# A hybrid encoder step on one core: second norm inside the output product, u tiles turned beside the queries, first norm between weight splits, bias line stored from ScalarE, four row buffers

## What is computed

```python
xn = rmsnorm(x, norm1_g)
z = xn @ w_in + b_in                      # split: attention q,k,v | mLSTM q,k,v | gates
x = x + merge(attention, mlstm, gates)    # two branch products, sigmoid gates, then @ w_out
xn = rmsnorm(x, norm2_g)
q = (xn @ peer_wq).reshape(n, 8, 2, 64)   # 8 heads, two sub keys each
s = einsum('nhpd,hpkd->nhpk', q, sub_keys)
fv, eidx = top_k of the 16 x 16 sums of the two top-16 lists    # 16 experts per head
h = gelu(u[eidx] . xn)                    # 16384 experts, u and v are 16384 x 1024
x = x + sum(softmax(fv) * h * v[eidx])
y = rmsnorm(x, final_g)
```

## Time and profile before

| | us |
|---|---|
| median of three runs | 1967.35 (1964.7 to 1967.36) |
| the profiled execution, its own time | 1964.37 |
| its span in the profile | 1962.5 |
| TensorE busy / VectorE / ScalarE / GpSimd | 1886.2 / 1371.4 / 873.8 / 848.8 |
| mean granted clock of TensorE | 0.987 |

### The profile page before, as it was taken

The page is one execution under the profiler, slowest core; times in us unless marked ns, Lnnn a source line. Parts: engine busy times, 40 slices in busy tenths (PEclk is TensorE's granted clock), DMA queues, the critical chain, the costliest instruction groups (busy, mean ns, idle before and its releaser), DMA issues. The chain is left out here.

```text
span 1962.5 us, 32250 instructions
## 1 busy us (share of the span) xinstructions
PE 1886.2 (96%) x11529; PEld 1799.0 (92%) x11529; DVE 1371.4 (70%) x2645; ACT 873.8 (45%) x1839; POOL 848.8 (43%) x670
## 2 busy tenths in 40 slices
PE   7999999998989999999999899999999999999998
PEld 6988878888979998999999899999999999999997
DVE  3126746667541898899999777775677787777775
ACT  4021122234131437688888778773333333333333
POOL 4425323331114359688888776651122222222210
PEclk9999999999989999999999999999999999999999
DMA  7632189987711445999999999999799999999982
GB/s 175 115 95 80 53 213 285 266 262 256 177 54 23 139 148 174 283 287 283 289 294 272 281 309 311 328 307 314 264 334 341 348 331 346 351 327 348 350 299 92
DMA packets 325954, 481.08 MB, mean 245 GB/s; under 512 B 37628, under 2 KB 250108, under 8 KB 322468
## 3 DMA queue, kind: packets, MB, share of 16 engines
q1 hardware_dynamic: 287724, 341.63, 56.9%
q0 software_dynamic: 36864, 134.23, 21.3%
q10 hardware_dynamic: 1208, 3.16, 0.4%
HBM read 393.81 MB, written 83.97 MB: 243 GB/s over the span
## 5 line engine op out<-in xcount | busy, mean ns | idle before, releaser
L1493 PE MATMUL ps<-x_high,split_high 128*128 128x416 f32 x1024 | 371.6, 363 | 20.6 <-DVE split_low L1480 17.9
L1493 PE MATMUL ps<-x_high,split_low 128*128 128x416 f32 x1024 | 362.9, 354 | 0.0
L1493 PE MATMUL ps<-x_low,split_high 128*128 128x416 f32 x1024 | 360.9, 352 | 0.0
L2140 PE MATMUL ps<-hid_high,split_high 128*128 128x416 f32 x1024 | 358.9, 350 | 1.5 <-PEq L1707 1.5
L2140 PE MATMUL ps<-hid_low,split_high 128*128 128x416 f32 x1024 | 358.8, 350 | 0.0
L2140 PE MATMUL ps<-hid_high,split_low 128*128 128x416 f32 x1024 | 358.7, 350 | 0.0
L1362 POOL DMA_INDIRECT gathered_rows<-in_peer_v_dram,gathered_index x128 | 134.3, 1049 | 419.6 <-DVE gathered_acc L1399 342.7
L2083 ACT CAST split_high<-area 128x1024 fp32r<-128x1024 f32 x127 | 133.3, 1049 | 383.5 <-PE ps L2140 382.7
L1684 POOL TENSOR_SCALAR area<-iota_row,chosen 128x128 f32<-128x128 f32 x240 | 287.9, 1206 | 2.1
L2111 DVE TENSOR_TENSOR split_low<-area,split_high 128x1024 fp32r<-128x1024 f32 x127 | 155.6, 1225 | 136.1 <-ACT split_high L2083 136.1
L1493 PEld LDWEIGHTS ps<-x_high,split_high 128*128 128x128 f32 x1024 | 194.0, 189 | 28.7 <-DVE split_low L1480 21.9
(11 more groups left out here) (293 smaller groups left out, 3782.4 us busy)
## 6 DMA issues: line engine op xcount, KB each, us to landing
area<-in_peer_v_dram SPq DMA_DIRECT2D x128, 512.0 KB, 5.5
u_nat<-in_peer_u_dram SPq DMA_DIRECT2D x392, 128.0 KB, 5.8
routing<-dense SPq DMA_DIRECT2D x26, 1024.0 KB, 7.2
area<-hidden SPq DMA_DIRECT2D x128, 208.0 KB, 7.1
hidden<-gelu_out SPq DMA_DIRECT2D x124, 208.0 KB, 5.1
w_raw<-in_w_in_dram SPq DMA_DIRECT2D x44, 512.0 KB, 6.1
mv_nat<-in_peer_u_dram SPq DMA_DIRECT2D x120, 128.0 KB, 3.6
u_nat<-turned_u SPq DMA_DIRECT2D x30, 512.0 KB, 3.7
```

Source lines behind the costliest of these rows:

```text
L1493: ins = self.nc.tensor.matmul(self.k.ps[:, b, 0:N], w[:, b, kk, :], x[:, kk, 0:N], start=(kk == 0 and p == 0), stop=(kk == KD - 1 and p == 2))
L2140: ins = nc.tensor.matmul(ps[:, kk, 0:N], v[:, b, kk * P:(kk + 1) * P], h[:, b, :], start=(n == 0 and p == 0), stop=(n == P - 1 and p == 2))
```

## The change

The order of `units` in the input product becomes: three tiles of x, the first product of mq, the other two tiles of x, three more products, then cache and bias line. ScalarE makes one tile's statistics after the other. The norm's weights are loaded as full rows, and the norm multiplies by them, so that turned halves need one copy and one subtraction each. Some constants are issued from ScalarE, and so are the eight stores of the bias line. In `merge` the units of the output product are ordered so that frame tiles become complete one after the other; VectorE normalises each, TensorE turns it two units later, ScalarE and VectorE split it, the splits of the first query weights stand between, and two query products are made at the block's end. In `queries` VectorE makes the low parts of the query weights, and eight more tiles of u (30 to 37) are loaded, turned and stored there. The routing matrices of ScalarE are made in place, without the tile `apart`. `RING` is 4 and `AHEAD` 38. Query weights and the split x lie at fixed places in memory.

```diff
-AHEAD = 30
+BESIDE_ATTENTION = 30
+AHEAD = BESIDE_ATTENTION + 8
...
-RING = 3
+RING = 4
...
-LOADS = QUARTERS + 2
+LOADS = 3
...
+QUERY_UNITS = [(0, 0), (1, 0), (0, 1), (1, 1)] + [(m, h) for m in range(2, PH) for h in range(2)]
+QUERIES_AHEAD = 2
...
+def query_weights_high(nc, k, pool, m):
+
+    if m % 4 == 0:
+        pool.wait_ge(k.wq_loaded[m // 4], 16 * QUARTERS)
+    if m >= 2:
+        pool.wait_ge(k.q_done, 1 + max(i for i, (b, _) in enumerate(QUERY_UNITS) if b == m - 2))
+    nc.gpsimd.tensor_copy(k.wq_high[:, m % 2], query_weights(k, m)).then_inc(k.wq_high_done, 1)
+
+
+def query_weights_low(nc, k, dve, m):
+
+    dve.wait_ge(k.wq_high_done, m + 1)
+    nc.vector.tensor_tensor(k.wq_low[:, m % 2], query_weights(k, m), k.wq_high[:, m % 2], ALU.subtract).then_inc(k.wq_low_done, 1)
...
+    def load(self, sp, n):
+
+        after(sp, self.k.u_turned, n - 1)
+        load_quarters(sp, self.nat[:, n % 2, :], self.peer_u, n, self.k.tile_loaded[3 + n % 2])
...
+    def turn(self, dve, n):
+        dve.wait_ge(self.k.tile_loaded[3 + n % 2], 16 + 16 * QUARTERS * (n // 2 + 1))
+        after(dve, self.k.u_stored[n % 2], 32 * (n // 2))
+        for i in range(2):
+            kk = slice(i * KD // 2, (i + 1) * KD // 2)
+            ins = self.nc.vector.transpose(self.turned[n % 2][i].bitcast(U32).rearrange("p (b g i) -> p g b i", b=KD // 2, i=BLK),
+                                           self.nat[:, n % 2, :].bitcast(U32).rearrange("p (g b j) -> p g b j", g=P // BLK, j=BLK)[:, :, kk, :])
+        ins.then_inc(self.k.u_turned, 1)
...
-    units = [("xn", (t, g), "vec") for t in range(NT) for g in range(2)]
-    units += [("cache", s, "act") for s in range(4)]
-    units += [("line", i, "act") for i in range(2)]
+    rest_of_x = [("xn", (t, g), "vec") for t in range(3, NT) for g in range(2)]
+    cache_and_line = [("cache", s, "act") for s in range(4)] + [("line", i, "act") for i in range(2)]
...
+        if c == 0:
+            units += new[0:1] + rest_of_x + [new[2], new[1], new[3]] + cache_and_line + new[4:]
...
+    STATISTICS_BEFORE = {("xn", (0, 0)): [0, 1, 2], ("mq", (0, 0, 0)): [3, 4]}
...
+            load_x(0)
+            sp.dma_start(g1_row, norm1_g[0].partition_broadcast(P)).then_inc(g1_loaded, 16)
+            load_x(1)
+            load_x(2)
+            load_tile(0)
+            load_x(3)
+            load_x(4)
+            load_tile(1)
+            sp.dma_start(kc_nat, cache_att_k[0, 0].rearrange("(s p) h d -> p s (h d)", p=P)).then_inc(cache_loaded, 16)
+            sp.dma_start(table[:, 0, :], att_rel_bias[0, 1:P + 1, :]).then_inc(tab_loaded, 16)
+            sp.dma_start(table[:, 1, :], att_rel_bias[0, P + 1:2 * P + 1, :]).then_inc(tab_loaded, 16)
...
-                if 5 <= i < 5 + PIECES:
-                    sp.wait_ge(line_done, 1)
-                    rows = slice((i - 5) * P // PIECES, (i - 4) * P // PIECES)
-                    sp.dma_start(k.line_dram[:, rows], bcast(line, 1, P // PIECES)).then_inc(line_stored, 16)
...
+            def statistics(t):
+                r = ROWS[t]
+                act.wait_ge(x_loaded[t], 16)
+                nc.scalar.activation(xn[0:r, t, :], x[0:r, t, :], ACT.Square, accum_out=k.ss[0:r, t:t + 1]).then_inc(k.squared, 1)
+                act.wait_ge(k.averaged, t + 1)
+                nc.scalar.activation(k.ss[0:r, t:t + 1], k.rstd[0:r, t:t + 1], ACT.Sqrt).then_inc(k.rooted, 1)
...
+                    act.dma_start(wg_raw[:, :, :], w_in[0, :, GATES:GA].rearrange("(k p) n -> p k n", p=P)).then_inc(wg_loaded, 16)
+                    act.wait_ge(tab_loaded, 48)
...
+                    nc.scalar.copy(xnT_high[:, 4 * g:4 * g + 4, t * P:t * P + r], turned_bank(u, r)).then_inc(high_out, 1)
+                if kind == "mk" and arg[1:] >= (1, 0):
+                    i = 2 * arg[1] + arg[2] - 2
+                    act.wait_ge(line_done, 1)
+                    act.dma_start(k.line_dram[:, i * P // PIECES:(i + 1) * P // PIECES], bcast(line, 1, P // PIECES)).then_inc(line_stored, 16)
+                if kind == "mv" and arg[1:] in ((0, 0), (0, 1)):
+                    i = 6 + arg[2]
+                    act.dma_start(k.line_dram[:, i * P // PIECES:(i + 1) * P // PIECES], bcast(line, 1, P // PIECES)).then_inc(line_stored, 16)
...
+                nc.vector.scalar_tensor_tensor(out=xn[0:r, t, :], in0=x[0:r, t, :], scalar=k.rstd[0:r, t:t + 1],
+                                               in1=g1_row[0:r, :], op0=ALU.mult, op1=ALU.mult).then_inc(normed, 1)
...
+    UNITS = [(i, t) for i in range(2) for t in range(NT)] + [(2, 0), (2, 1), (3, 0), (3, 1)] + [(i, t) for t in range(2, NT) for i in (2, 3)]
+    OUTS = len(UNITS)
+    ends = [UNITS.index((3, t)) for t in range(NT)]
...
+                elif c == CHUNKS - 1:
+                    pool.wait_ge(summed, 2 * KD)
+                    for m in range(2):
+                        query_weights_high(nc, k, pool, m)
+                    pool.wait_ge(out_done, NT * (c - 1 - CHUNKS // 2))
...
+            def turn(t):
+                r = ROWS[t]
+                pe.wait_ge(x_normed, t + 1)
+                for g in range(2):
+                    b = (2 * t + g) % 4
+                    after(pe, k.x_low_done, 2 * t + g - 3)
+                    for i in range(4):
+                        kk = 4 * g + i
+                        ins = nc.tensor.transpose(ps[:, b, i * P:i * P + r], xn[0:r, t, kk * P:(kk + 1) * P], ident[0:r, 0:r])
+                    ins.then_inc(k.frames_turned, 1)
+
...
+                if u - 2 in ends[0:4]:
+                    turn(ends.index(u - 2))
+            pe.wait_ge(k.x_low_done, 6)
+            for i in range(QUERIES_AHEAD):
+                pe.wait_ge(out_added, OUTS - 3 + i)
+                query(nc, k, pe, i)
+                if i == 0:
+                    turn(NT - 1)
...
+                if t >= 1:
+                    r = ROWS[t - 1]
+                    for g in range(2):
+                        act.wait_ge(k.frames_turned, 2 * (t - 1) + g + 1)
+                        nc.scalar.copy(k.x_high[:, 4 * g:4 * g + 4, (t - 1) * P:(t - 1) * P + r], turned_bank(t - 1, g)).then_inc(x_high_done, 1)
...
+                for a in range(QUARTERS):
+                    cols = slice(a * D // QUARTERS, (a + 1) * D // QUARTERS)
+                    ins = nc.vector.scalar_tensor_tensor(out=xn[0:r, t, :].rearrange("r (b a j) -> r a b j", b=KD, a=QUARTERS)[:, a],
+                                                         in0=x[0:r, t, cols].rearrange("r (b j) -> r b j", b=KD), scalar=k.rstd[0:r, t:t + 1],
+                                                         in1=g2_row[0:r, cols].rearrange("r (b j) -> r b j", b=KD), op0=ALU.mult, op1=ALU.mult)
+                ins.then_inc(x_normed, 1)
...
+                if u in (NT + 2, NT + 3):
+                    query_weights_low(nc, k, dve, u - NT - 2)
+                if u in ends:
+                    norm(ends.index(u))
+                if u == ends[2]:
+                    x_low(0)
+                if u > ends[2] and u % 2 == 0:
+                    x_low(1 + (u - ends[2]) // 2)
...
-                nc.gpsimd.tensor_tensor(w_low[:, m % 2], raw, w_high[:, m % 2], ALU.subtract
-                                        ).then_inc(w_low_done, 1)
+            for m in range(2, PH):
+                query_weights_high(nc, k, pool, m)
...
+            for n in range(BESIDE_ATTENTION, AHEAD):
+                ahead.store(sp, n)
+                if n + 2 < AHEAD:
+                    ahead.load(sp, n + 2)
...
+            later = list(range(BESIDE_ATTENTION, AHEAD))
+            for m in range(4, PH):
+                for n in later[2 * (m - 4):2 * (m - 3)]:
+                    ahead.turn(dve, n)
+                query_weights_low(nc, k, dve, m)
...
-                    after(act, second_ready, b - 1)
-                    if b - 2 in plan.on_scalar:
-                        act.wait_ge(scalar_first_ready, sum(i <= b - 2 for i in plan.on_scalar))
+                    after(act, routed, b - AREAS + 1)
                     for f in range(FEW):
                         c = plan.column(b) + f
-                        ins = nc.scalar.activation(apart[:, b % 2, f, :], iota[:, :], ACT.Abs, bias=chosen[:, 1, c:c + 1])
+                        ins = nc.scalar.activation(second[:, b % AREAS, f, :], iota[:, :], ACT.Abs, bias=chosen[:, 1, c:c + 1])
```

More of the change, by code:

```diff
@@ new lines, with query, query_weights @@
+QUERIES_AHEAD = 2
+def query(nc, k, pe, i):
+    m, h = QUERY_UNITS[i]
+    pe.wait_ge(k.wq_low_done, m + 1)
+    for kk in range(KD):
+        for p, (w, x) in enumerate(((k.wq_high, k.x_high), (k.wq_high, k.x_low), (k.wq_low, k.x_high))):
+            ins = nc.tensor.matmul(k.ps[:, 4 + i % 4, 0:HALF], w[:, m % 2, kk, :], x[:, kk, h * HALF:(h + 1) * HALF],
+                                   start=(kk == 0 and p == 0), stop=(kk == KD - 1 and p == 2))
+    ins.then_inc(k.q_done, 1)
+def query_weights(k, m):
+    return k.wq[m // 4][:, :, (m % 4) * P:(m % 4 + 1) * P]
```

(29 more changed lines are left out.)

283 lines of the change are left out of this document (124 added, 159 removed).

## The result

The changed kernel takes **1983.72 us** (median of four, 1980.44 to 1984.56) against 1966.95 before, a ratio of 1.0086 with a 95% interval of 1.0070 to 1.0102: slower by some 17 us, where 1938 was forecast. The profiled execution took 1982.97 us for a span of 1981.2; before it was 1962.5, so 18.7 us are to be found.

A forecast was written before the change was run, and what follows sets the result against it. The prediction took TensorE to bound the kernel, with idle time to win in three places. Start 4.0, output product to queries 12.4 and search 10 sum to 26.4: 1964.4 - 26.4 = 1938 us, range 1929 to 1947.

The forecast's parts named there:

- the bias line's stores: Input product: moving the eight stores from SP to ScalarE wins 2.3 us, or 0 if the transfer is the limit.
- the rival that ended slower: Queries: u-tile loads landing over 13.8 us make the kernel slower; at 16, stall 38.9 and 1975 us; chance 0.03.
- The order of the start: Start: new load order, moved stores and clock loss together win 4.0 us, between -1 and +8.
- the bias column: Start: ScalarE, waiting for it till about 22.5, evicts the first product at 23.5; the second starts at 24.8.
- the low pace: Start: thin work from 20 to 25 us lowers the granted clock; 1.0 us taken off the gain.
- Output product and queries: From output product to end of queries: 114.3 us instead of 126.7, winning 12.4, from 6 to 15.
- the stall from the tiles of u: Queries: weight splits wait behind u tiles, costing 2.0 us; 0 if loads land in 2, 8.3 at 5.8.
- The round: Queries: half turns, stores and loads of u take 7.6 us per round against TensorE's 6.0.
- The search: Search: less TensorE idle time wins 10 us; ends 0 and all 23.7.
- The two reliefs: Search: eight turns leave VectorE (9.9 us), and four row buffers shorten its gather waits (10 us).
- the capped sum: Search: relief of 17.7 us exceeds TensorE's 14.5 idle in 800 to 1098; two thirds of that, 10, taken.
- The rival that the gathers are bound by the DMA engines: Search: gathers limited by DMA engines, not by when they leave, so the search gains nothing: 1948 us; chance 0.22.

The follow-up runs named there:

- experiment 2: The kernel before, with only the eight bias-line stores moved from SP to ScalarE: 2007.75 us, ratio 1.0206.
- experiment 7: The changed kernel, with the bias line stored once from ScalarE and its copies made memory to memory on SP between weight tiles 17 and 24: 1939.97 us.
- experiments 1 and 6: 1: the changed kernel with the eight stores back on SP, 1950.13 us; 6: that kernel with thirty tiles ahead instead of 38, 1948.09 us.
- experiment 8: The kernel of experiment 7, with the sub keys' load ahead of the eight quarter loads of u on SP: 1936.74 us, ratio 0.9860.
- the square: The kernel of experiment 8 with tiles ahead and row buffers varied: 38, 4: 1939.00 us; 30, 4: 1940.14; 38, 3: 1944.86; 30, 3: 1942.51.
- the four kernels with a burst: The changed kernel (1983.72 us), experiment 2, the changed kernel with stores cut into rows of 192 columns (1966.21 us), and experiment 4.
- experiment 4: The changed kernel, with each store on ScalarE waiting for a weight tile's high part: 1963.79 us, ratio 0.9975.

## Why the prediction was wrong, step by step

**The step that failed: the bias line's stores.** The prediction said "A free SP issues a load in 0.50, so I hold the issue and not the transfer to be the limit, and the 2.3 us go; were it the transfer, 0." It was the transfer, and 0 was no bound. Moved to a second queue, the stores lost their place in SP's order, in which each load stood behind one store at most, and became a burst of 61 us on eight engines. The first load that was issued into it stood still till 65 us, and then it and the next went packet for packet with the stores. The step gave -2.3 and measured +39.7 in the kernel before (2007.75 - 1968.09 on the same chip, experiment 2). The row was there: each store had held SP for 5.06 us, ten times the 0.50 of a load; and in the same trace a store and a load came every 8.07 us (stores issued at 60.89 and 68.96), 0.9 MB where the start moved 0.27 MB per us and would have needed 3.3:

```profile
60.89 5.18 SPq L477 DMA_DIRECT2D rel_line<-work  x1
67.67 1.25 SPq L452 DMA_DIRECT2D w_raw<-in_w_in_dram  x1
68.96 5.45 SPq L477 DMA_DIRECT2D rel_line<-work  x1
```

The question left out was what a load on one queue does while another queue is full. None of the rivals had this place; the rival that ended slower had another chain. The prediction cites a rule of the Trainium skill (DMA: Bandwidth & Descriptors, Rules for kernel authors) that spreading gains no bandwidth; it is the rule on taking turns, on the same page, that speaks against the change.

**The order of the start**: right in its times, and in part by luck. The fourth mq product ends when the turns of the cache begin, and the next product starts at 36.29; 36.2 was forecast, against 38.9 before. Timeline of TensorE in the changed kernel, and of ScalarE's first eviction:

```profile
17.26 0.56 PE L441 MATMUL ps<-xnT_high,w_high 128*128 128x272 f32 x1 [1.52 <-DVE xnT_low L786]
...
21.70 0.43 PE L441 MATMUL ps<-xnT_low,w_high 128*128 128x272 f32 x1
21.93 0.43 PE L441 MATMUL ps<-xnT_high,w_low 128*128 128x272 f32 x1
...
25.01 0.29 PE L441 MATMUL ps<-xnT_low,w_high 128*128 128x272 f32 x1
25.13 0.29 PE L441 MATMUL ps<-xnT_high,w_low 128*128 128x272 f32 x1
...
33.91 1.91 PE L982 MATMUL ps<-ident,mv_nat 128*128 128x128 f32 x16
...
36.29 0.39 PE L441 MATMUL ps<-xnT_high,w_high 128*128 128x272 f32 x1
...
22.97 0.49 ACT L654 ACTIVATE mqT<-ps,b_col 128x272 f32<-128x272 f32 x1 [2.81 <-PE ps L441]
```

The first product starts at 17.26 for 16.7, and the second at 24.8 as forecast, but for another reason. ScalarE was to hold it, with its statistics, an issue and the bias column; in fact ScalarE waits 2.81 us for the product itself. Its 24 matmuls start 0.23 us apart till 22.4 and take 5.4 us, where those of the second start 0.13 apart: 272 columns in 0.226 us are the pace of 1.2 GHz. The column of the granted clock says 1.00 for that stretch, but the trace's first record of the clock is at 22.5. So the low pace came earlier than the 20 to 25 us of the prediction and cost up to 2.4 us, not 1.0, and the bias column did not hold the product. With the stores out of the way (experiment 7) the stage won 5.9 where 4.0 was said.

**Output product and queries**: -12.4 forecast, -5.4 measured. The norms are hidden as worked out: with thirty tiles ahead the stretch is 112.2 to the last query matmul, and the sum without the stall was 112.3 to the block's end, some 0.7 later. What was mis-sized is the stall from the tiles of u: 2.0 said, and 8.5 us is the difference of experiments 1 and 6, of which 6.2 are waits and some 1.8 a lower clock (0.91 from 640 to 660 in the changed kernel). The round was right (7.6 said, 7.0 to 7.2 measured in experiment 8); its start was not. The timeline of VectorE, and TensorE's first wait:

```profile
633.26 1.27 DVE L1729 SCALAR_TENSOR_TENSOR gathered_x<-x,rstd,g_row 32x1024 f32<-32x1024 f32 x1 [4.98 <-DMA gathered_rows<-in_peer_sub_keys_dram]
634.57 3.25 DVE L1733 SCALAR_TENSOR_TENSOR gathered_x<-x,rstd,g_row 32x1024 f32<-32x1024 f32 x2
637.85 1.22 DVE L259 TENSOR_TENSOR wq_low<-area,wq_high 128x1024 fp32r<-128x1024 f32 x1
...
639.22 0.36 PE L237 MATMUL ps<-x_high,wq_high 128*128 128x272 f32 x1 [3.39 <-DVE wq_low L259]
```

The eight quarter loads of u were put ahead of the sub keys on SP; the scaling of the gathered frames waits for the keys, and the split of the next query weights, now on VectorE, stands behind it. A moved load was costed in the round, but not for what it does to the loads behind it in its queue. With the keys first the chain of tiles alone still had 5.1 us of waits (experiment 8), so 2.0 was too little in either order.

**The search**: -10 forecast, -15.6 in the changed kernel's profile, -12.1 in that of experiment 7, and 9.5 between the corners of the square. Idle time of TensorE fell from 25.4 us (724.9 - 699.5, from 640.5 to 1365.4) to 16.2 (709.7 - 693.54), and its busy time by 6.0, with the granted clock at 1.00 instead of 0.99. The two reliefs were named rightly and the capped sum was near; that busy time would fall too was not in it. The rival that the gathers are bound by the DMA engines falls: the waits for them went from 68.1 to 15.4 at the same share of 0.89.

**The sum.** With the stores out of the way the forecast was near: 1939.97 in experiment 7 for 1938. In part that is luck, since errors cancel: a start 2 us and a search 2 us better than said, and the queries 7 worse.

## What to carry to other kernels

A transfer that moves to another engine's queue leaves the order it stood in. Before it is moved, take its time on the DMA engines, not its issue, and work out what the loads of the old queue do while it lasts. Here the first stood still until the stores issued before it were through, and then the loads went on packet for packet, packets of 512 bytes at the pace of 3 KB packets. In this kernel it was better to make the slow store small and its copies where nothing waits for them (one store of 24 KB, the copies from memory 60 to 140 us later) than to move it to a free engine.

## What the hardware showed that was not expected

- A DMA out of eight partitions of SBUF: 168 packets of 3 KB in 10 us at 46.2% of sixteen engines, so 0.44 us of an engine for 3 KB. Cut into 768 bytes it was 0.11 us a packet (40.3% of sixteen engines for 297 packets in 5 us), the same for each byte. In experiment 7 the copies of the same 384 KB from memory to memory came in stretches of some 200 GB/s in all, against 58 in the changed kernel from 70 to 80.
- Two queues on the same eight engines were served one packet each, at 3 KB against 512 bytes (168 to 168 in 10 us) and at 768 against 512 bytes (297 to 299 in 5 us).
- The turns do not begin at once: in the four kernels with a burst the first load stood still on the stores' engines until about the end of the second store (none of its packets from 61 to 65 in the changed kernel, from 60 to 64 in experiment 4). Two stores had been issued before it each time; the reason is not shown.
